# A two-layer encoder trunk on one core: three kinds of transposes issued later

## The chip, the cores and the metric

The kernel runs on one core of one Trainium2 chip. The metric is the device time of one execution in microseconds (us), from the core's first to its last work; lower is better.

## The reference

Two layers of a bidirectional encoder over 256 tokens of width 1024, all in float32. Each layer:

```
h = rms_norm(x)
c_q, c_kv, k_rope, dq, dk, dv = split(h @ w_in)
o_a = mla_attention(...)     # 8 heads: softmax of (q_nope k_nope + q_rope k_rope), times v
o_b = diff_attention(...)    # 8 heads: softmax map 1 minus lambda times softmax map 2, times v
merged = sigmoid(h @ w_gate)[a] * (o_a @ w_branch_a) + sigmoid(...)[b] * (o_b @ w_branch_b)
x = x + merged @ w_out
h = rms_norm(x)
x = x + swiglu(h)                      # layer 0: dense, 2816 wide
x = x + top-2-of-8 expert swiglu(h)    # layer 1: each expert 3584 wide
```

## The kernel before

**Weights in two parts.** Weights stream from HBM in float32, 1 MB at a time: 'pieces' (ring of 6 buffers) in attention and the dense layer, 'granules' (ring of 14) in the expert layer. Each is split on the chip into a high part (ScalarE copies it, `hi`, L1114; `high`, L1493) and a low part (VectorE subtracts, `lo`, L1603; `low`, L2201). A product is three matmuls of 128 x 512 per block of 128 rows of the contraction: high x high, low x high, high x low (`three`, L551 for pieces, L968 for granules). There are 4 high buffers for pieces and 6 for granules, and a high buffer is free again when TensorE has used it.

**Five queues written by hand.** TensorE, ScalarE, VectorE, GpSimd and the DMA queue of SyncE each have their own program, in which the instructions stand in a fixed order and wait on semaphores. TensorE's results lie in eight PSUM banks; `bank_table` gives every result, in advance, a bank and a number in that bank's order. A result may be written when the bank's earlier user has been read (`take`: wait for `free[bank]`); who reads it last drains its engine and then frees the bank (`gave`, L1101 on ScalarE, L1589 on VectorE). Transposed things use the banks trans0 and trans1 in turn, in the order of the list `turned`.

**The attention loop.** After a first part, TensorE runs steps u = 1 to 15 for 16 heads (u below 8: the first attention; from 8: the differential one). Step u: scores of head u; first half of a projection (`half(u, 0)`, 12 matmuls); transposes of head u - 1's probabilities (`turn_prob`, job W(u-1)); second half of the projection; then `weigh(u - 1)`, the product of turned probabilities and values, into bank ctx (job C). ScalarE in step u: copies or squares from the step before, one `hi`, the exponentials of head u (`exps`), the copy of the turned probabilities out of PSUM (`turned_prob(u - 1)`, L1244). VectorE: `low_oa` (L1846), the row maxima (`top`), one `lo`, the division (`weights`).

**The later heads' operands.** Queries and keys for the later heads (qn1, dq1, dk1) are projected inside this loop, scaled by VectorE into the buffer zb, and then turned by TensorE in two jobs of four 128 x 128 transposes each (a and b, through `turn_z`, which calls `turn`; the transposes are at L583). ScalarE copies both out (`turned_op`, L1204). Before, both jobs stand in one step directly behind W(u-1): qn1 in u = 2, dq1 in u = 4, dk1 in u = 8. Job b has the same bank as W(u-1).

**The expert loop.** Rows routed to an expert are gathered by a matrix G of ones and zeros, and the result is scattered by its transpose S. An expert has 7 chunks; step s: `project(0, s)` (gate, granules first_gran(s) and the next), transposes of the hidden chunk before (`turn`, L1002), `project(1, s)` (up, two granules), `down(s - 1)` (two granules). Each of the three is 24 matmuls. Step 0 has no turn and no down and uses granules 0 to 3; step 1 uses 4 to 7 for the projections and 8 and 9 for down. VectorE's order in step s is: low of the two down granules, low of the next step's first, `turned(s - 1)` (L2207, which down(s - 1) waits for), low of the second, low of the third, `hidden` (L2216), low of the fourth. Steps 0 and 1 of the first expert stand ahead of the loop. Between them TensorE computes the slot columns (L546, `first_columns`; VectorE reads them at L2161 and L2162 and drains at L2163) and turns G (`scatter_matrix`, L956), both in bank proj2; ScalarE copies S (L1483) in the same place. S is first used at the first expert's end.

Of the kernel before, what the change touches and what calls it, by code (L numbers as in the profile page):

```python
# [100 lines left out]
def bank_table():  # L101

    jobs, used = {}, {b: 0 for b in BANKS}

    def put(l, bank, *names):
        for name in names:
            jobs[l, name] = (bank, used[bank])
            used[bank] += 1

    def turns(l, which):  # L110
        put(l, "trans0", which + "0")
        put(l, "score0", which + "1")
        put(l, "trans0", which + "2")
        put(l, "score1", which + "3")

    for l in range(DEPTH):
        turns(l, "x")
        put(l, "proj0", "cq.0", "qr.0", "kn1.0")
        put(l, "proj1", "cq.1", "qr.1", "kn1.1")
        put(l, "proj2", "kv.0", "dk0.0", "qn0.0", "dv0.0")  # L120
        put(l, "ctx", "kv.1", "dk0.1", "qn0.1", "dv0.1", *(f"C{u}" for u in range(2 * HEADS)), "b0.1", "o1.0")
        put(l, "score0", "dq0.0", "v0.0", "v1.0", "kn0.0")
        put(l, "score1", "dq0.1", "v0.1", "v1.1", "kn0.1")
        for h in range(HEADS):
            put(l, f"score{h % 2}", f"S{h}")
        for d in range(HEADS):
            put(l, "score0", f"E{d}.0")
            put(l, "score1", f"E{d}.1")
        n = 2
        for name in ("qn1", "dq1", "dv1", "dk1", "g0", "g1", "g2", "g3", "a0"):  # L130
            for t in range(TT):
                put(l, f"proj{n % 3}", f"{name}.{t}")
                n += 1
        put(l, "proj2", "a1.0")
        put(l, "score0", "a1.1")
        put(l, "score1", "b0.0")
        put(l, "proj0", "b1.0")
        put(l, "proj1", "b1.1")
        put(l, "proj2", "o1.1")
        turned = ["KV", "KR", "cqa", "cqb", "dq0a", "dq0b", "dk0a", "dk0b", "qn0a", "qn0b", "qra", "qrb", "kn0a",  # L140
                  "kn0b", "kn1a", "kn1b"]
        for u in range(2 * HEADS):
            turned += [f"W{u}"] + {1: ["qn1a", "qn1b"], 3: ["dq1a", "dq1b"], 7: ["dk1a", "dk1b"]}.get(u, [])
        turned += ["ob0", "ob1", "ob2", "ob3", "m0", "m1", "m2", "m3"]
        for n, name in enumerate(turned):
            put(l, f"trans{n % 2}", name)
        put(l, "score0", "o0.0")
        put(l, "score1", "o0.1")
        turns(l, "f")
        if l % 2 == 0:  # L150
            n = 0
            for c in range(FF_CHUNKS):
                for m in "gu":
                    for t in range(TT):
                        put(l, f"proj{n % 3}", f"ff{m}{c}.{t}")
                        n += 1
                put(l, "trans0", *(f"h{c}.{j}" for j in range(2 if c < FF_CHUNKS - 1 else 1)))
            put(l, "score0", "acc0.0")
            put(l, "score1", "acc0.1")
            put(l, "trans1", "acc1.0")  # L160
            put(l, "ctx", "acc1.1")
        else:
            put(l, "trans1", "logit")
            put(l, "proj2", "rank")
    return jobs, used
# [10 lines left out]
def along(k, rnd, per_rnd, e=0, per_e=0):  # L176
    v = k
    for reg, per in ((rnd, per_rnd), (e, per_e)):
        v = v + reg * per if isinstance(reg, int) else reg * per + v
    return v  # L180
# [25 lines left out]
def bank_use(bank, k, rnd, e=0):  # L206
    per_rnd, per_e = MOE_USES[bank]
    return along(MOE_START[bank] + k, rnd, per_rnd, e, per_e)
# [5 lines left out]
def build(nc, x_rows, pos_row, pos_col, const, gains, lam_vecs, w_pre, ffn_row, w_router, w_exp, out, h_rows):  # L214
    with ExitStack() as ctx:
# [307 lines left out]
        def _(pe):  # L523
# [79 lines left out]
            def turn_z(l, z, job, blocks):  # L603
                if z == "qr":
                    pe.wait_ge(rotated_q, l + 1)
                else:
                    pe.wait_ge(scaled, nth(SCALED, l, z))
                turn(l, job, blocks_of(zbuf(l, z), blocks))
# [4 lines left out]
            def attention(l):  # L613
# [33 lines left out]
                def turn_both(name):  # L647
                    turn_z(l, name, name + "a", (0, 1))
                    turn_z(l, name, name + "b", (2, 3))
# [40 lines left out]
                def weigh(u):  # L690

                    pe.wait_ge(probT_ready, l * 2 * HEADS + u + 1)
                    o = open_(l, f"C{u}")
                    if u < HEADS:
                        pe.wait_ge(value, nth(VALUES, l, f"v{u // 4}.1"))
                        for k in range(TT):
                            m = mm(o[:, 0:T], blk(v_mla[:, k], u), probT[:, u % 2, k], k, TT)
                    else:
                        d = u - HEADS
                        pe.wait_ge(value, nth(VALUES, l, f"dv{d // 4}.1"))  # L700
                        for q in range(TT):
                            for k in range(TT):
                                m = mm(o[:, q * P:(q + 1) * P], probT[:, u % 2, k, q * P:(q + 1) * P],
                                       blk(v_diff[:, k], d), k, TT)
                    m.then_inc(full["ctx"], 1)
# [62 lines left out]
                def half(u, part):  # L768
                    name, t = beside[u - 1]
                    proj(name, part, t, rows_of.get(name, h))  # L770

                last = 2 * HEADS - 1
                for u in range(1, last + 1):
                    if u >= HEADS:
                        scores(u)
                    elif u % 2 == 0:
                        pair_scores(u)
                    if u == last:
                        pe.wait_ge(oa_ready, l * HEADS + HEADS)
                    half(u, 0)  # L780
                    turn_prob(u - 1)
                    for v, name in ((2, "qn1"), (4, "dq1"), (8, "dk1")):
                        if u == v:
                            turn_both(name)
                    half(u, 1)
                    weigh(u - 1)
                half(last + 1, 0)
                turn_prob(last)
# [163 lines left out]
            def scatter_matrix(value):  # L952

                o = take("proj2", value)
                for t in range(TT):
                    m = nc.tensor.transpose(o[:, t * P:(t + 1) * P], G[:, t], c_("ident"))  # L956
                m.then_inc(full["proj2"], 1)
# [9 lines left out]
            def experts(rnd):  # L967
# [81 lines left out]
                def first_columns():  # L1049
                    slot_columns(along(1, rnd, EXPERTS), bank_use("proj2", 0, rnd))  # L1050
# [6 lines left out]
                step(0, 0)  # L1057
                if first_round(rnd):
                    first_columns()
                scatter_matrix(bank_use("proj2", 1, rnd))  # L1060
                step(1, 0)
                with pe.Fori(0, EXPERTS - 1) as e:
                    for s in range(2, EXP_CHUNKS + 2):
                        step(s, e)
# [27 lines left out]
        def _(act):  # L1092
# [126 lines left out]
            def attention(l):  # L1219
# [116 lines left out]
                for u in range(1, 2 * HEADS):  # L1336
                    if 2 <= u < HEADS + 2:
                        high_oa(u - 2)
                    if u >= HEADS + 2:
                        ob_sums(u - 2 - HEADS)  # L1340
                    if u == 1:
                        squares(l, "qn1")
                    if u in (2, 3):
                        squares(l, "dq1", (u - 2,))
                    if u in (4, 5):
                        diff_values(1, u - 4)
                    if u in (6, 7):
                        squares(l, "dk1", (u - 6,))
                    if u >= HEADS:
                        gate_rows((u - HEADS) // TT, u % TT)  # L1350
                    hi(at + 16 + u)
                    for v, name in ((1, "qn1"), (3, "dq1"), (7, "dk1")):
                        if u == v:
                            roots_of(l, name)
                    exps(u)
                    turned_prob(u - 1)
                    if u == 2:
                        turned_op(l, "qn1", qnT, "qn", 4)
                    if u == 4:
                        turned_op(l, "dq1", dqT, "dq", 4)  # L1360
                    if u == 8:
                        turned_op(l, "dk1", dkT, "dk", 4)
                last = 2 * HEADS - 1
                ob_sums(HEADS - 2)
# [115 lines left out]
            def scatter_matrix(value):  # L1480

                o = fresh("proj2", value)
                A(S[:], o[:, 0:T], ACT.Copy).then_inc(scatter_ready, 1)  # L1483
                act.drain().then_inc(free["proj2"], 1)

            def experts(rnd):
# [56 lines left out]
                gathered(lambda bank: bank_use(bank, 0, rnd))  # L1543
                high(3, 0)
                step(0, 0)
                scatter_matrix(bank_use("proj2", 1, rnd))
                step(1, 0)
                with act.Fori(0, EXPERTS - 1) as e:
                    for s in range(2, EXP_CHUNKS + 2):
                        step(s, e)  # L1550
# [898 lines left out]
```

## Time and profile before

| | |
|---|---|
| median of 3 runs | 1805.65 us (1804.97 to 1808.34) |
| the profiled execution | 1804.76 us, span of its instructions 1802.9 us |
| matmuls (PE) | 1743.7 us busy, 97% of the span |
| weight loads (PEld, beside the matmuls) | 1433.7 us, 80% |
| VectorE (DVE) | 1416.0 us, 79% |
| ScalarE (ACT) | 1175.9 us, 65% |
| GpSimd (POOL) | 28.5 us, 2% |
| mean granted TensorE clock | 0.990 of full speed |
| read from HBM | 477 MB, 266 GB/s over the span |

A row of a timeline gives start, duration, engine, line of the kernel, operation, output and inputs with the program's names, shapes, and how many instructions are merged in it; in brackets, the engine's idle time before it and what ended that. ACTq and DVEq are the two engines' queues, here their drains. Times are counted from the first instruction.

### The profile page before, as it was taken

The page shows a single profiled execution, that of the slowest core. Times are in us where ns is not written, and L with a number is a line of the kernel's source. Part 1 is how long each engine was busy: PE and PEld are TensorE (multiplying, and loading weights), DVE is VectorE, ACT ScalarE, POOL GpSimd, SP SyncE. Part 2 cuts the span into 40 slices and gives each one's busy share as a digit, 9 for nine tenths or more (in the row PEclk, how much of TensorE's full clock was granted, in tenths as well). Part 3 has the DMA queues.
Part 4 walks back from the last instruction along what each step waited for, and adds up shares of the span by engine and source line. Part 5 has one row for each costly group of instructions (what it writes and reads, how often), then busy time and mean ns, then how long its engine had stood idle before and what let it go on. Part 6 is the DMA issues. An engine that isn't in the chain of part 4 may idle for free.

```text
span 1802.9 us, 23755 instructions
## 1 busy us (share of the span) xinstructions
PE 1743.7 (97%) x8220; PEld 1433.7 (80%) x8220; DVE 1416.0 (79%) x1423; ACT 1175.9 (65%) x1242; POOL 28.5 (2%) x27
## 2 busy tenths in 40 slices
PE   7999999999999999988999999999999999999997
PEld 6777878888887778776888888888888888888885
DVE  7776876544478668668889889898898998988984
ACT  7655665434466656646777777777777777777772
POOL 0200000000002000000000000000000000000000
PEclk9999999999999999989999999999999999999998
DMA  7433345555454324577999999999999999999980
GB/s 281 164 117 117 117 142 186 187 191 185 166 187 164 117 94 141 222 284 294 375 376 356 376 358 355 381 355 370 367 357 380 373 354 377 352 369 371 361 318 25
DMA packets 68408, 480.50 MB, mean 267 GB/s; under 512 B 7920, under 2 KB 8176, under 8 KB 11248
## 3 DMA queue, kind: packets, MB, share of 16 engines
q1 hardware_dynamic: 67328, 475.91, 71.0%
q0 software_dynamic: 1008, 3.67, 0.6%
q8 instruction: 41, 0.67, 0.1%
q14 instruction: 31, 0.25, 0.0%
HBM read 477.45 MB, written 2.10 MB: 266 GB/s over the span
## 4 chain that ended last, share of the span: by engine, by line
PE 77%; DVE 8%; issue 5%; ACT 4%; DVEq 4%; ACTq 1%; DMA 1%; SPq 0%
PE ps_proj L970 9%; PE ps_proj L974 9%; PE ps_proj L973 9%; PE ps_proj L552 7%; PE ps_proj L554 7%; PE ps_proj L555 7%; PE ps_score L970 5%; PE ps_score L974 5%; PE ps_score L973 5%; DVE w_raw_r L2201 3%; PE ps_score L546 2%; PE ps_trans L583 2%; PE ps_ctx L546 2%; PE ps_score L552 1%; PE ps_score L555 1%
## 5 line engine op out<-in xcount | busy, mean ns | idle before, releaser
L2201 DVE TENSOR_TENSOR w_raw_r<-w_raw,hi 128x2048 fp32r<-128x2048 f32 x336 | 759.3, 2290 | 95.1 <-ACT hi L1493 74.3
L1493 ACT ACTIVATE hi<-w_raw 128x2048 fp32r<-128x2048 f32 x335 | 639.6, 1919 | 183.3 <-PE ps_score L974 72.1
L970 PE MATMUL ps_proj<-hi,he_hi 128*128 128x512 f32 x896 | 355.3, 397 | 0.1
L974 PE MATMUL ps_proj<-w_raw_r,he_hi 128*128 128x512 f32 x896 | 350.1, 391 | 0.0
L973 PE MATMUL ps_proj<-hi,he_lo 128*128 128x512 f32 x896 | 349.6, 390 | 0.0
L1114 ACT ACTIVATE hi<-raw 128x2048 fp32r<-128x2048 f32 (+1 forms) x114 | 215.8, 1893 | 124.8 <-PE ps_proj L554 60.6
L1603 DVE TENSOR_TENSOR raw_r<-raw,hi 128x2048 fp32r<-128x2048 f32 (+1 forms) x114 | 257.2, 2266 | 33.3 <-ACT hi L1114 27.0
L552 PE MATMUL ps_proj<-hi,hT_hi 128*128 128x512 f32 (+2 forms) x496 | 198.2, 400 | 6.6 <-DVEq L1589 3.5
L974 PEld LDWEIGHTS ps_proj<-w_raw_r,he_hi 128*128 128x128 f32 x896 | 168.5, 188 | 36.1
L970 PEld LDWEIGHTS ps_proj<-hi,he_hi 128*128 128x128 f32 x896 | 168.7, 188 | 34.9 <-issue 1.5
L973 PEld LDWEIGHTS ps_proj<-hi,he_lo 128*128 128x128 f32 x896 | 168.8, 188 | 33.4
L555 PE MATMUL ps_proj<-raw_r,hT_hi 128*128 128x512 f32 (+2 forms) x496 | 190.2, 383 | 0.0
L554 PE MATMUL ps_proj<-hi,hT_lo 128*128 128x512 f32 (+2 forms) x496 | 189.9, 383 | 0.0
L970 PE MATMUL ps_score<-hi,hidT_hi 128*128 128x512 f32 x448 | 176.0, 393 | 1.6 <-DVE hidT_lo L2207 1.6
L974 PE MATMUL ps_score<-w_raw_r,hidT_hi 128*128 128x512 f32 x448 | 174.6, 390 | 0.0
L973 PE MATMUL ps_score<-hi,hidT_lo 128*128 128x512 f32 x448 | 174.4, 389 | 0.0
L552 PEld LDWEIGHTS ps_proj<-hi,hT_hi 128*128 128x128 f32 x496 | 94.2, 190 | 31.4 <-issue 12.9
L555 PEld LDWEIGHTS ps_proj<-raw_r,hT_hi 128*128 128x128 f32 x496 | 93.9, 189 | 18.7
L554 PEld LDWEIGHTS ps_proj<-hi,hT_lo 128*128 128x128 f32 x496 | 94.3, 190 | 15.9
L970 PEld LDWEIGHTS ps_score<-hi,hidT_hi 128*128 128x128 f32 x448 | 84.1, 188 | 19.2 <-DVE hidT_lo L2207 2.3
L974 PEld LDWEIGHTS ps_score<-w_raw_r,hidT_hi 128*128 128x128 f32 x448 | 84.1, 188 | 17.7
L973 PEld LDWEIGHTS ps_score<-hi,hidT_lo 128*128 128x128 f32 x448 | 84.2, 188 | 17.1
(347 smaller groups left out, 2000.7 us busy)
## 6 DMA issues: line engine op xcount, KB each, us to landing
w_raw<-in_w_exp SPq DMA_DIRECT2D x336, 1024.0 KB, 6.7
raw<-in_w_pre SPq DMA_DIRECT2D x110, 1024.0 KB, 4.9
raw<-in_w_pre SPq DMA_DIRECT2D x4, 640.0 KB, 6.0
x_tok<-in_x_rows SPq DMA_DIRECT2D x2, 512.0 KB, 4.9
raw<-in_w_pre SPq DMA_DIRECT2D x2, 512.0 KB, 5.9
h_rows<-htok SPq DMA_DIRECT2D x1, 1024.0 KB, 8.2
out_rows<-x_tok SPq DMA_DIRECT2D x1, 1024.0 KB, 4.1
grow<-in_ffn_row SPq DMA_DIRECT2D x1, 512.0 KB, 5.7
```

The lines of the kernel that those rows point to most:

```text
L546: m = nc.tensor.matmul(o, lhsT, rhs, start=(k == 0), stop=(k == n - 1))
L552: m = nc.tensor.matmul(o, x_h, w_h, start=first, stop=False)
L554: m2 = nc.tensor.matmul(o, x_l, w_h, start=False, stop=False)
L555: return m2, nc.tensor.matmul(o, x_h, w_l, start=False, stop=last)
L583: m = nc.tensor.transpose(o[:, b * P:(b + 1) * P], src, c_("ident"))
L970: m = nc.tensor.matmul(o, a_hi, w_h, start=first, stop=False)
L973: nc.tensor.matmul(o, a_lo, w_h, start=False, stop=False)
L974: return nc.tensor.matmul(o, a_hi, w_l, start=False, stop=last)
L1114: A(high[g % HIGH][:, 0:w], raw[g % RAW][:, 0:w], ACT.Copy).then_inc(piece_hi, 1)
L1493: A(w_hi[k % HS][:], w_raw[n], ACT.Copy).then_inc(gran_hi, 1)
L1603: V.tensor_tensor(low[g % RAW][:, 0:w], raw[g % RAW][:, 0:w], high[g % HIGH][:, 0:w].bitcast(F32), ALU.subtract).then_inc(piece_lo, 1)
L2201: V.tensor_tensor(w_low[k % WS], w_raw[k % WS], w_hi[k % HS][:].bitcast(F32), ALU.subtract)\
```

## The change

Three edits. In the attention loop, job b of a turned chunk moves from before the second half of the step's projection to behind it, for qn1, dq1 and dk1 alike. Both jobs of dk1, and their copies on ScalarE, move from u = 8 to u = 9, and their place in the banks' order with them. In the expert part, TensorE's turn of G and ScalarE's copy of S move from between steps 0 and 1 to behind step 1. No instruction is added or removed.

```diff
--- before.py
+++ after.py
@@ -140,7 +140,7 @@
         turned = ["KV", "KR", "cqa", "cqb", "dq0a", "dq0b", "dk0a", "dk0b", "qn0a", "qn0b", "qra", "qrb", "kn0a",
                   "kn0b", "kn1a", "kn1b"]
         for u in range(2 * HEADS):
-            turned += [f"W{u}"] + {1: ["qn1a", "qn1b"], 3: ["dq1a", "dq1b"], 7: ["dk1a", "dk1b"]}.get(u, [])
+            turned += [f"W{u}"] + {1: ["qn1a", "qn1b"], 3: ["dq1a", "dq1b"], 8: ["dk1a", "dk1b"]}.get(u, [])
         turned += ["ob0", "ob1", "ob2", "ob3", "m0", "m1", "m2", "m3"]
         for n, name in enumerate(turned):
             put(l, f"trans{n % 2}", name)
@@ -779,10 +779,12 @@
                         pe.wait_ge(oa_ready, l * HEADS + HEADS)
                     half(u, 0)
                     turn_prob(u - 1)
-                    for v, name in ((2, "qn1"), (4, "dq1"), (8, "dk1")):
-                        if u == v:
-                            turn_both(name)
+                    turned = {2: "qn1", 4: "dq1", 9: "dk1"}.get(u)
+                    if turned:
+                        turn_z(l, turned, turned + "a", (0, 1))
                     half(u, 1)
+                    if turned:
+                        turn_z(l, turned, turned + "b", (2, 3))
                     weigh(u - 1)
                 half(last + 1, 0)
                 turn_prob(last)
@@ -1057,8 +1059,8 @@
                 step(0, 0)
                 if first_round(rnd):
                     first_columns()
+                step(1, 0)
                 scatter_matrix(bank_use("proj2", 1, rnd))
-                step(1, 0)
                 with pe.Fori(0, EXPERTS - 1) as e:
                     for s in range(2, EXP_CHUNKS + 2):
                         step(s, e)
@@ -1358,7 +1360,7 @@
                         turned_op(l, "qn1", qnT, "qn", 4)
                     if u == 4:
                         turned_op(l, "dq1", dqT, "dq", 4)
-                    if u == 8:
+                    if u == 9:
                         turned_op(l, "dk1", dkT, "dk", 4)
                 last = 2 * HEADS - 1
                 ob_sums(HEADS - 2)
@@ -1543,8 +1545,8 @@
                 gathered(lambda bank: bank_use(bank, 0, rnd))
                 high(3, 0)
                 step(0, 0)
+                step(1, 0)
                 scatter_matrix(bank_use("proj2", 1, rnd))
-                step(1, 0)
                 with act.Fori(0, EXPERTS - 1) as e:
                     for s in range(2, EXP_CHUNKS + 2):
                         step(s, e)
```

## Rows read from the trace of the kernel before

**Rows 1.** stretches of the span: busy us of each engine (instructions), granted clock, DMA share, GB/s
```profile
84.00:90.00 6.00, 5.60 (x29) 4.76 (x30) 4.40 (x5) 2.17 (x5) 0.78 (x1) 1.00 0.54 178
...
176.00:179.80 3.80, 3.10 (x10) 2.65 (x11) 1.88 (x7) 1.89 (x4) 0.00 (x0) 0.55 0.19 78
...
900.00:1790.00 890.00, 885.58 (x4034) 728.72 (x4033) 788.37 (x506) 649.64 (x441) 5.62 (x6) 1.00 0.92 350
```

**Rows 2.** TensorE's waits: for whom, us in total, times, longest
```profile
PE ps_trans L583 <- ACTq L1101: 8.1, 6, 3.3
...
PE ps_proj L956 <- DVEq L2163: 7.3, 1, 7.3
```

**Rows 3.** timeline of TensorE, layer 0: start us, us, instruction [idle before, releaser]
```profile
84.40 0.47 PE L552 MATMUL ps_proj<-hi,hT_hi 128*128 128x512 f32 x1 [1.80 <-DVEq L1589]
```

**Rows 4.** timeline of TensorE, layer 0, u = 8 and the scores of u = 9
```profile
172.37 0.60 PE L583 MATMUL ps_trans<-cst,prob 128*128 128x128 f32 x4
...
176.70 1.09 PE L583 MATMUL ps_trans<-cst,zb 128*128 128x128 f32 x4 [3.29 <-ACTq L1101]
...
181.33 1.02 PE L546 MATMUL ps_ctx<-probT,v_mla 128*128 128x256 f32 x4
...
182.29 1.14 PE L546 MATMUL ps_score<-dkT,dqT 64*128 64x256 f32 x8
```

**Rows 5.** timeline of ScalarE and VectorE, layer 0, u = 8 and 9
```profile
175.94 0.57 ACT L1244 ACTIVATE probT<-ps_trans 128x512 f32<-128x512 f32 x1
...
182.39 0.38 ACT L1249 ACTIVATE oaT_hi<-ps_ctx 128x256 fp32r<-128x256 f32 x1 [3.88 <-PE ps_ctx L546]
...
182.88 0.42 DVE L1846 TENSOR_TENSOR oaT_lo<-ps_ctx,oaT_hi 128x256 fp32r<-128x256 f32 x1 [4.85 <-ACT oaT_hi L1249]
...
188.45 0.58 ACT L1244 ACTIVATE probT<-ps_trans 128x512 f32<-128x512 f32 x1
```

**Rows 6.** timeline of TensorE, layer 0, u = 9: W8 and weigh(8)
```profile
186.21 0.60 PE L583 MATMUL ps_trans<-cst,dprob 128*128 128x128 f32 x4
...
189.40 1.05 PE L546 MATMUL ps_ctx<-v_diff,probT 128*128 128x128 f32 x8
```

**Rows 7.** timeline of TensorE and ScalarE, layer 0, u = 2
```profile
121.74 0.60 PE L583 MATMUL ps_trans<-cst,zb 128*128 128x128 f32 x4
...
122.72 0.63 PE L583 MATMUL ps_trans<-cst,zb 128*128 128x128 f32 x4 [0.38 <-ACTq L1101]
...
123.10 0.47 PE L552 MATMUL ps_proj<-hi,hT_hi 128*128 128x512 f32 x1
...
126.99 0.38 ACT L1249 ACTIVATE oaT_hi<-ps_ctx 128x256 fp32r<-128x256 f32 x1 [2.85 <-PE ps_ctx L546]
```

**Rows 8.** timeline of TensorE, the experts' steps 0 and 1
```profile
817.70 0.50 PE L546 MATMUL ps_proj<-pair,G 128*128 128x2 f32 x4
...
825.48 0.69 PE L956 MATMUL ps_proj<-cst,G 128*128 128x128 f32 x2 [7.28 <-DVEq L2163]
...
838.44 0.39 PE L970 MATMUL ps_score<-hi,hidT_hi 128*128 128x512 f32 x1
...
843.88 0.39 PE L970 MATMUL ps_proj<-hi,he_hi 128*128 128x512 f32 x1
```

**Rows 9.** timeline of VectorE, the experts' steps 0 and 1
```profile
815.54 6.69 DVE L2201 TENSOR_TENSOR w_raw_r<-w_raw,hi 128x2048 fp32r<-128x2048 f32 x3
...
822.97 2.29 DVE L2201 TENSOR_TENSOR w_raw_r<-w_raw,hi 128x2048 fp32r<-128x2048 f32 x1
...
828.77 6.70 DVE L2201 TENSOR_TENSOR w_raw_r<-w_raw,hi 128x2048 fp32r<-128x2048 f32 x3 [3.10 <-ACT hi L1493]
...
835.39 0.68 DVE L2207 TENSOR_TENSOR hidT_lo<-ps_trans,hidT_hi 128x512 fp32r<-128x512 f32 x1
...
841.44 6.89 DVE L2201 TENSOR_TENSOR w_raw_r<-w_raw,hi 128x2048 fp32r<-128x2048 f32 x3
```

**Rows 10.** timeline of ScalarE, the experts' step 0
```profile
813.17 5.52 ACT L1493 ACTIVATE hi<-w_raw 128x2048 fp32r<-128x2048 f32 x3
```

## Prediction

> **What bounds the kernel now.** I read the page's table of engines first: matmuls cover 97% of the span, VectorE 79%, ScalarE 65%. Then a table of stretches: between 900 and 1790 us TensorE is busy 885.6 of 890 us at full granted clock, VectorE 788, while the DMA engines are busy 0.92 of the time [rows 1]. So almost every microsecond is TensorE's own work, and a change that removes no matmul can only win where TensorE stands still or runs at the lower of its two clocks (1.2 instead of 2.4 GHz). The list of TensorE's waits says where that is: six waits of the zb and probability transposes for a ScalarE drain, 8.1 us together, the longest 3.3, and one of 7.3 us of the scatter matrix for VectorE [rows 2]. The diff touches just these. In the whole trace no engine waits for DMA but the first transposes for x, so time saved early isn't lost to loading later.
>
> A wait costs more than its length if it lowers the clock. After the 3.29 us wait the granted clock is 0.55 for 3.8 us; after one of 1.80 us it stays 1.00 [rows 1, 3].
>
> **The chunk dk1, u = 8 (once in each layer; layer 0 shown, layer 1 has the same 3.29 us).** Before: W7 is turned at 172.37, dk1a 0.43 us later, then dk1b needs the bank that W7 holds. ScalarE copies W7 only after the four exponentials of step 8, at 175.94 for 0.57 us, and dk1b starts at 176.70. weigh(7) starts at 181.33 and the scores of step 9 at 182.29 [rows 4, 5].
> After, u = 8 has no dk1. A turn of W and a half projection behind it take 189.40 - 186.21 = 3.19 us at full clock [rows 6], so TensorE is at weigh(7) at 172.37 + 3.19 = 175.56. weigh(7) reads the same copy, which is there at 176.51, say 176.6 with its handover: a new wait of 1.0 us, below the 1.80 that kept the clock. Then 0.96 us of weigh (182.29 - 181.33), and the scores of step 9 start at 177.56: 4.73 us earlier. That is the 3.29, 1.4 us of slow clock (176.70 to 182.29 is 5.59 us, where 0.38 + 2.83 + 0.96 = 4.17 would do, the 0.38 from [rows 7]) and one turn, less the new 1.0.
>
> u = 9 gets both turns. Everything on ScalarE and VectorE there starts from weigh(7): ScalarE sat idle 3.88 us before its copy of C7, VectorE 4.85 us before low_oa(7), so it was free from 178.03; moved up by 4.73 us that instruction starts at 178.15, which just fits [rows 5]. W8 is turned at 181.48, dk1a follows (+0.43), then the half projection: 181.48 + 0.43 + 3.19 = 185.1, and TensorE is at dk1b. dk1b needs W8's bank: its copy at 188.45 + 0.58 becomes 184.3. So it doesn't wait, by 0.8 us. The two turns add 0.43 + 0.38 = 0.8 us. ScalarE copies dk1b by about 186.2, under weigh(8), and then would wait for weigh(8)'s output anyway. Net 4.73 - 0.8 = 3.9 us per layer, **7.8 us** for both. The heads of dk1 are read first at u = 12, three steps later. Nothing of this issues a DMA; SP's queue waits for used pieces and follows TensorE.
> Bounds: if the 1.0 us wait also cost the clock, 1.2 to 1.4 us less per layer (11.4 us as the total below); if it were nil, 1.0 more per layer.
>
> **qn1 at u = 2 and dq1 at u = 4 (four places in both layers).** Before, the first turn starts at 121.74, the second at 122.72 (after 0.38 us of wait for W1's bank), and the projection at 123.10: 1.36 us. Apart, each turn costs 0.38 us, 0.76 together, and the second finds its bank free, which it came to be at 122.7. Saved 0.6 us. The cost is that ScalarE stands in its queue for the second turn until about 125.4 and copies it until 126.1; it was idle 2.85 us before 126.99, waiting for weigh(1), which comes behind that turn and takes 0.9 us, so the copy lies under it [rows 7]. dq1 shows the same times. 4 x 0.6 = **2.4 us**; bounds 0 (the copy of 0.69 us lands on ScalarE's path each time) and 2.6.
>
> **The scatter matrix.** Before, TensorE ends step 0 with the columns product at 817.70 and waits 7.28 us, to 825.48, for the drain behind VectorE's slot_columns, which VectorE reaches only after granules 4 to 7. Then the first projection of step 1, and down(0) starts at 838.44, step 2 at 843.88 [rows 8].
> After, TensorE goes straight into step 1 at about 818.1. Its granules: VectorE makes 4, 5 and 6 in three instructions from 815.54 (done 817.8, 820.0, 822.2), and 7 from 822.97 to 825.26 [rows 9]. A projection is 24 matmuls like down(0), which takes 843.88 - 838.44 = 5.44 us. The first runs to 823.6, the turn to 823.9, the second to 829.4, none of it late. down(0) then waits for turned(0) on VectorE. That stood at 835.39 for 0.68 us, behind granules 8 to 10, which began at 828.77 after 3.10 us of idling for ScalarE's copy of granule 8. ScalarE had ended its copies 5 to 7 at 813.17 + 5.52 = 818.69 and then stood at the scatter matrix, which TensorE turns at 825.48 [rows 8 to 10]; now it goes on at once, so VectorE loses just those 3.10 us and turned(0) ends at 836.07 - 3.10 = 832.97. So **the wait isn't removed but half of it moves to down(0): 829.4 to 833.0, 3.6 us**. down(0) takes its 5.44 us, the scatter matrix 0.38.
> Without loss of clock step 2 starts at 833.0 + 5.44 + 0.38 = 838.8, 5.1 us earlier. But 3.6 us is more than the 3.29 us that cost 1.4 us in both layers, so I take that: 840.2, a gain of **3.7 us**.
> The Trainium skill (TensorE: Matmul & The Clock Gate, section on the HAM clock gate) says that the gate's observation is free-running, not aligned with the kernel; by that a wait near the edge may escape, and the sum would be 5.1. The two equal rows here don't show such an escape.
> What is late next: ScalarE's copy of S now stands behind step 1, so granule 14 waits for TensorE's scatter turn: free at 840.6, copies 14 to 16 until 846.4. VectorE then makes 14, 15, 16 by 849.3 and turned(1) by 850.0. TensorE wants it at 840.2 + 5.46 + 0.44 + 5.46 = 851.5: 1.5 us to spare, where before it was over 3 (four granules from 841.44 and turned(1), about 851.7, against 843.88 + 11.3 = 855.2). VectorE has 788 of 890 us to do in the loop [rows 1], so it gains some 1.5 us per step and the margin grows. SP's refills wait for gran_done, so they too come earlier; they run at 350 GB/s with no consumer waiting. GpSimd's first gather needs the second index, far later.
>
> **Sum.** 7.8 + 2.4 + 3.7 = 13.9 us. The profiled execution took 1804.76 us (span 1802.9): 1790.9. It lies 0.9 us under the median of the runs, 1805.65, so I forecast **1791.7**, 0.8% faster. No change can be told within 0.2%, or 3.6 us.
>
> **The rivals.**
> 1. *No clock is lost at down(0)*, the wait of 3.6 us escaping: 5.1 for 3.7, 1790.3. For it: nothing between 1.8 and 3.29 us was seen. Against: 3.29 did cost, twice.
> 2. *The new wait at weigh(7) is longer or lowers the clock*: 2.5 to 2.9 us less, and with the copies of qn1 and dq1 on ScalarE's path up to 2.4 less, 1794 to 1797. For it: low_oa(7) fits by only 0.1 us, dk1b by 0.8. Against: the 1.80 us wait at full clock.
> 3. *The gain is spent again in the expert loop*: granule 14 is late, VectorE's margin of 1.5 us is gone and TensorE waits at down(1), down(2) until VectorE has caught up. If copies or handovers are 2 us later than I have it, some 1 to 3 us come back: 1793 to 1795.
> 4. *Slower*: the expert loop settles in a worse order, in which TensorE waits for turned() in each step because ScalarE waits for TensorE. Over the 55 steps left it takes 0.25 us per step to eat 13.9 us; 0.4 us per step would give 1814. For it: each of the three engines waits for the next one. Against: VectorE's 100 us of spare time in the loop [rows 1], which is more than 1.5 us a step.
> 5. *Nothing*: the waits are only moved to the next dependency in all places, as happens to half of the scatter wait: 1803 to 1806. Against: weigh(7) depends on one copy whose time is on the trace.
>
> **How the numbers follow.** Forecast with rival 1, which differ by 1.4 us: 0.68. Rival 2: 0.12; rival 3: 0.11; rival 5: 0.04; rival 4: 0.03; something else, either side, 0.02. Both signs don't share the chance, so one range: downward no new wait at weigh(7) and no lost clock (2.0 + 1.4 us, and 0.9 us for the runs), 1787.5; upward rivals 2 and 3, 1797.5. Faster by over 0.2%: 0.93; within: 0.04; slower: 0.03.
>
> **What will show it.** Right: no wait of a zb transpose for a ScalarE drain; TensorE idle about 1.0 us before ps_ctx of weigh(7) in both layers, clock kept; scores of step 9 near 176.4 (177.56 less 1.2 us of the earlier turns); no wait of 7 us at the scatter matrix, but one of 3.6 us of ps_score (down) for hidT_lo with a clock of about 0.5 behind it; the expert loop as long as before. Wrong: a wait at dk1b in u = 9, ScalarE late at oaT_hi, hidT_lo waits in steps 2 to 4, or a loop that is longer from step to step.

## The result

The changed kernel takes 1791.88 us (median of 4 runs, 1789.35 to 1794.02) against 1805.31 us (4 runs, 1803.53 to 1808.34): ratio 0.992, 95% interval 0.9908 to 0.9932. That is 13.4 us faster. The forecast was 1791.7 us. The profiled execution has a span of 1787.5 us, 15.4 less than the one before. It is the fastest of the four.

TensorE's waits after, of the whole span. The two groups of [rows 2] are gone, and two others are new or longer:

```profile
PE ps_score L972 <- DVE hidT_lo L2209: 5.3, 3, 3.7
...
PE ps_ctx L546 <- ACT probT L1246: 1.7, 2, 0.9
```

The copy of the turned probabilities is waited for once in each layer, 0.85 us, and hidT_lo at down(0) for 3.66 us (its other two waits, 1.6 us together, are the ones of the kernel before).

TensorE in layer 0, u = 8 and 9, its transposes, scores and weigh (these answer to [rows 4, 6]):

```profile
171.27 0.60 PE L583 MATMUL ps_trans<-cst,prob 128*128 128x128 f32 x4
...
175.48 1.13 PE L546 MATMUL ps_ctx<-probT,v_mla 128*128 128x256 f32 x4 [0.85 <-ACT probT L1246]
...
176.54 1.14 PE L546 MATMUL ps_score<-dkT,dqT 64*128 64x256 f32 x8
...
180.47 0.60 PE L583 MATMUL ps_trans<-cst,dprob 128*128 128x128 f32 x4
...
180.90 0.60 PE L583 MATMUL ps_trans<-cst,zb 128*128 128x128 f32 x4
...
184.11 0.60 PE L583 MATMUL ps_trans<-cst,zb 128*128 128x128 f32 x4
...
184.54 1.06 PE L546 MATMUL ps_ctx<-v_diff,probT 128*128 128x128 f32 x8
```

W7 is turned at 171.27 and nothing stands between it and the half projection. weigh(7) waits 0.85 us, the scores of u = 9 start at 176.54. W8 is turned at 180.47, dk1a at 180.90, dk1b at 184.11 without a wait.

ScalarE and VectorE there, against [rows 5]:

```profile
174.85 0.57 ACT L1246 ACTIVATE probT<-ps_trans 128x512 f32<-128x512 f32 x1
...
176.64 0.38 ACT L1251 ACTIVATE oaT_hi<-ps_ctx 128x256 fp32r<-128x256 f32 x1 [1.22 <-PE ps_ctx L546]
...
177.13 0.42 DVE L1848 TENSOR_TENSOR oaT_lo<-ps_ctx,oaT_hi 128x256 fp32r<-128x256 f32 x1 [0.20 <-ACT oaT_hi L1251]
...
182.69 0.57 ACT L1246 ACTIVATE probT<-ps_trans 128x512 f32<-128x512 f32 x1
...
184.75 0.69 ACT L1206 ACTIVATE dkT<-ps_trans,gn 128x512 f32<-128x512 f32 x1 [0.68 <-PE ps_trans L583]
```

ScalarE's copies of W7 and W8 end at 175.42 and 183.26, VectorE reaches low_oa(7) with 0.20 us to spare instead of 4.85, and ScalarE copies dk1b under weigh(8).

u = 2 in layer 0, TensorE and then ScalarE, against [rows 7]:

```profile
125.08 0.60 PE L583 MATMUL ps_trans<-cst,zb 128*128 128x128 f32 x4
...
125.52 1.03 PE L546 MATMUL ps_ctx<-probT,v_mla 128*128 128x256 f32 x4
...
125.72 0.69 ACT L1206 ACTIVATE qnT<-ps_trans,gn 128x512 f32<-128x512 f32 x1 [2.23 <-PE ps_trans L583]
...
126.58 0.39 ACT L1251 ACTIVATE oaT_hi<-ps_ctx 128x256 fp32r<-128x256 f32 x1 [0.18 <-PE ps_ctx L546]
```

The second job stands alone at 125.08, weigh(1) follows 0.44 us later, and ScalarE, busy with the copy until 126.4, is still 0.18 us early for the output of weigh(1). That margin was 2.85.

TensorE at the experts' steps 0 and 1, against [rows 8]: the columns product, down(0) and the start of step 2.

```profile
807.64 0.50 PE L546 MATMUL ps_proj<-pair,G 128*128 128x2 f32 x4
...
823.33 0.47 PE L972 MATMUL ps_score<-hi,hidT_hi 128*128 128x512 f32 x1 [3.66 <-DVE hidT_lo L2209]
...
829.03 0.48 PE L972 MATMUL ps_proj<-hi,he_hi 128*128 128x512 f32 x1
```

VectorE and ScalarE there, against [rows 9, 10]:

```profile
815.78 6.69 DVE L2203 TENSOR_TENSOR w_raw_r<-w_raw,hi 128x2048 fp32r<-128x2048 f32 x3
...
822.39 0.68 DVE L2209 TENSOR_TENSOR hidT_lo<-ps_trans,hidT_hi 128x512 fp32r<-128x512 f32 x1
...
832.00 6.70 DVE L2203 TENSOR_TENSOR w_raw_r<-w_raw,hi 128x2048 fp32r<-128x2048 f32 x3 [1.26 <-ACT hi L1495]
...
838.61 0.68 DVE L2209 TENSOR_TENSOR hidT_lo<-ps_trans,hidT_hi 128x512 fp32r<-128x512 f32 x1
...
803.11 10.93 ACT L1495 ACTIVATE hi<-w_raw 128x2048 fp32r<-128x2048 f32 x6
...
829.31 0.39 ACT L1485 ACTIVATE S<-ps_proj 128x256 fp32r<-128x256 f32 x1 [3.50 <-PE ps_proj L958]
```

ScalarE makes its six high copies without a stop, VectorE goes from granule 7 to granules 8 to 10 with no idle time, and turned(0) ends at 823.07. From the columns product to step 2 it takes 21.39 us instead of 26.18. VectorE waits 1.26 us for granule 14, whose copy stands behind that of S, and turned(1) still ends at 839.3, before TensorE's down(1), which starts at 840.5.

Two stretches after; the columns are those of [rows 1]. The first holds the wait at down(0), and the clock stays 1.00. The second is the expert loop, TensorE busy 880.6 of 885 us: nothing is given back there.

```profile
806.00:831.00 25.00, 21.34 (x99) 17.34 (x99) 24.06 (x16) 16.11 (x12) 0.00 (x0) 1.00 0.82 311
...
890.00:1775.00 885.00, 880.59 (x4010) 724.65 (x4009) 784.61 (x504) 645.41 (x438) 5.64 (x6) 1.00 0.92 350
```

### The profile page after: what moved, and what is told of

Same layout as the page of the kernel before. It is cut to its first block, busy times and chain, and to the rows that moved or that the text cites. A ratio compares the mean times of both kernels' runs of the same rounds, so it can differ in the third digit from the quotient of the medians.

```text
span 1787.5 us, 23755 instructions
## 1 busy us (share of the span) xinstructions
PE 1738.2 (97%) x8220; PEld 1429.4 (80%) x8220; DVE 1415.6 (79%) x1423; ACT 1175.3 (66%) x1242; POOL 28.5 (2%) x27
## 4 chain that ended last, share of the span: by engine, by line
PE 77%; DVE 8%; issue 5%; ACT 4%; DVEq 4%; ACTq 1%; DMA 1%; SPq 0%
PE ps_proj L972 9%; PE ps_proj L976 9%; PE ps_proj L975 9%; PE ps_proj L552 7%; PE ps_proj L555 7%; PE ps_proj L554 7%; PE ps_score L972 5%; PE ps_score L976 5%; PE ps_score L975 5%; DVE w_raw_r L2203 3%; PE ps_score L546 2%; PE ps_trans L583 2%; PE ps_ctx L546 2%; PE ps_score L552 1%; PE ps_score L555 1%
```

## The experiments

Every experiment was timed beside the kernel before, 4 to 8 times, and profiled once. In the tables 'to step 2' is the time from the columns product to the start of step 2, and 'down(0)' from its first matmul to step 2. Where the scatter matrix is turned behind step 1, that is down(0), 5.44 us in the trace before, and its two transposes.

### Each part alone

The attention edits alone: in the changed kernel the scatter matrix goes back between steps 0 and 1, in both TensorE's and ScalarE's program.

```diff
-                step(1, 0)
                 scatter_matrix(bank_use("proj2", 1, rnd))
+                step(1, 0)
```

> The changed kernel with the scatter matrix back between steps 0 and 1, so only the attention edits are made. By my sum these are worth 10.0 us (the two traces show 5.0 and 5.1 us per layer), so about 10 us faster than the kernel before, with the 7.3 us wait at the scatter matrix and its slow clock back. Rival (the time is given back in the expert part): under 7 us.

The scatter matrix alone: the kernel before with this edit, in both programs.

```diff
-                scatter_matrix(bank_use("proj2", 1, rnd))
                 step(1, 0)
+                scatter_matrix(bank_use("proj2", 1, rnd))
```

> The kernel before with only the scatter matrix moved behind step 1. If the wait of 3.6 us at down(0) costs the clock, 3.7 us faster than before; if it does not, 4.8 to 5.1 us. Rival (the parts are not independent, the expert part gains only because it starts in another phase): the two parts alone do not add up to the whole, 13.4 us, within 2 us.

| kernel | median us | ratio to before (95%) |
|---|---|---|
| before, same chip | 1805.71 | |
| attention edits alone | 1795.9 | 0.9941 (0.9928 to 0.9953) |
| scatter matrix alone | 1802.31 | 0.9977 (0.9966 to 0.9987) |

By the medians 9.8 and 3.4 us, together 13.2, against 13.4 for the whole. The intervals leave 8.5 to 13.0 and 2.3 to 6.1 us, so within the noise the parts add up, and no loss of the attention part in the expert part shows. In the trace of the scatter matrix alone down(0) starts like this:

```profile
833.67 0.77 PE L970 MATMUL ps_score<-hi,hidT_hi 128*128 128x512 f32 x1 [3.65 <-DVE hidT_lo L2207]
...
834.23 0.63 PE L973 MATMUL ps_score<-hi,hidT_lo 128*128 128x512 f32 x1
...
841.78 0.48 PE L970 MATMUL ps_proj<-hi,he_hi 128*128 128x512 f32 x1
```

The wait is the same as in the changed kernel, 3.65 us. But here the matmuls behind it are 0.43 us apart instead of 0.23, the lower clock, and down(0) to step 2 takes 8.11 us instead of 5.70.

### The clock at down(0)

The changed kernel was run unaltered two more times.

> The changed kernel again, unaltered, for a second profile and more times. Forecast by my sum: the wait at down(0) of 3.6 us lowers the clock in some executions, then down(0) to step 2 takes about 7.2 us instead of the 5.7 us of the first profile. Rival: a wait of that length never costs the clock, and it takes 5.7 us again.

> The changed kernel once more, for a direct comparison and a third profile of down(0): with its clock kept, 21.4 us from the columns product to step 2; lost, 23.8 us. Three of five profiles with a wait of 3.6 us have lost it wholly or in part, so 1791 to 1792 us as the median either way.

Median 1791.35 us (ratio 0.9917, 0.9905 to 0.993) and 1791.64 us (0.9912, 0.9896 to 0.9927). down(0) and step 2 in the first of them:

```profile
825.06 0.47 PE L972 MATMUL ps_score<-hi,hidT_hi 128*128 128x512 f32 x1 [3.65 <-DVE hidT_lo L2209]
...
830.76 0.48 PE L972 MATMUL ps_proj<-hi,he_hi 128*128 128x512 f32 x1
```

and in the second, with one row inside:

```profile
825.25 0.47 PE L972 MATMUL ps_score<-hi,hidT_hi 128*128 128x512 f32 x1 [3.63 <-DVE hidT_lo L2209]
...
826.25 0.39 PE L975 MATMUL ps_score<-hi,hidT_lo 128*128 128x512 f32 x1
...
826.47 0.58 PE L976 MATMUL ps_score<-w_raw_r,hidT_hi 128*128 128x512 f32 x1
...
832.58 0.48 PE L972 MATMUL ps_proj<-hi,he_hi 128*128 128x512 f32 x1
```

In the first the clock is kept, 5.70 us. In the second the first five matmuls run at full clock, the sixth and those behind it at half: 7.33 us, and 22.99 us to step 2. Over all six profiles with this wait:

| profile | wait us | down(0) us | to step 2 us |
|---|---|---|---|
| changed kernel | 3.66 | 5.70 | 21.39 |
| again | 3.65 | 5.70 | 21.37 |
| third time | 3.63 | 7.33 | 22.99 |
| scatter matrix alone | 3.65 | 8.11 | 23.78 |
| dk1 in u = 8 (below) | 3.65 | 8.13 | 23.80 |
| dk1's jobs together (below) | 3.62 | 7.12 | 22.76 |

The same wait costs nothing, 1.4 to 1.6 us, or 2.4 us. Between 3.62 and 3.66 us the length doesn't decide.

The same chance stands in a shorter wait, near the start of layer 0, in all kernels here: that of [rows 3]. In the first profile of the changed kernel, and then in the second:

```profile
84.54 0.47 PE L552 MATMUL ps_proj<-hi,hT_hi 128*128 128x512 f32 x1 [1.80 <-DVEq L1591]
```

```profile
84.55 0.47 PE L552 MATMUL ps_proj<-hi,hT_hi 128*128 128x512 f32 x1 [1.85 <-DVEq L1591]
...
86.42 0.63 PE L554 MATMUL ps_proj<-hi,hT_lo 128*128 128x512 f32 x1
```

with, in the second, this stretch (columns of [rows 1], granted clock 0.50):

```profile
86.00:88.00 2.00, 2.00 (x6) 1.61 (x5) 2.00 (x2) 0.00 (x0) 0.00 (x0) 0.50 1.00 295
```

In the first the clock stays at 1.00, and from this matmul to the next scores (at 99.48) it takes 14.94 us; in the second it falls after five matmuls and takes 16.53, in the third 16.63. Over the 13 profiles of this document the wait measures 1.78 to 1.86 us; it left the clock in five (the kernel before is one) and lowered it in eight. This accounts, to some 0.3 us, for how the three profiles of the unaltered kernel differ: the span is 1787.5 us with no loss at either wait, 1789.4 with a loss here alone, and 1791.1 with a loss here and at down(0).

To see what a longer wait at down(0) does, VectorE got extra work ahead of granule 8, additions into a buffer whose content is overwritten later:

```diff
+                    if s == 1:
+                        for _ in range(2):
+                            V.tensor_tensor(y_lo[:], x_tok[:, 0], x_tok[:, 1], ALU.add)
+                            dve.drain()
                     if s:
                         low(down0, e)
```

> The changed kernel with two additions of 128 x 1024 (and a drain each, about 2.4 us together) on VectorE before granule 8, with a result nobody reads. The wait at down(0) grows to about 6 us. If the clock is lost there by chance at 3.65 us (kept in two profiles, lost in two), at 6 us it should always be lost: 2.4 us more plus 2.4 us of slow clock, so 3 to 5 us slower than the changed kernel. If the length does not matter: 2.4 us slower, and the clock sometimes kept. If VectorE's work there is hidden after all: no change.

Median 1795.61 us (0.9941, 0.9927 to 0.9954), about 4 us above the changed kernel's 1791.35 to 1791.88. The wait grew to 6.18 us and the slow clock is there from the first matmul:

```profile
828.26 0.76 PE L972 MATMUL ps_score<-hi,hidT_hi 128*128 128x512 f32 x1 [6.18 <-DVE hidT_lo L2209]
...
836.58 0.47 PE L972 MATMUL ps_proj<-hi,he_hi 128*128 128x512 f32 x1
```

8.32 us from down(0) to step 2. The two additions take 2.5 us and the wait is 2.5 us longer, so VectorE's work ahead of turned(0) sets this wait microsecond by microsecond. One profile can't show that the clock is always lost at 6 us. Of the 4 us, 2.5 are the work; that the other 1.5 are a clock lost more often or for longer is an estimate from the difference.

### Which of the two attention edits brings the gain

dk1 back in u = 8, its second job still behind the half projection:

```diff
-        ... 8: ["dk1a", "dk1b"]
+        ... 7: ["dk1a", "dk1b"]
-                    turned = {2: "qn1", 4: "dq1", 9: "dk1"}.get(u)
+                    turned = {2: "qn1", 4: "dq1", 8: "dk1"}.get(u)
-                    if u == 9:
+                    if u == 8:
                         turned_op(l, "dk1", dkT, "dk", 4)
```

> The changed kernel with dk1 back in u = 8, but its second job still behind the half projection. Theory A (the delay of dk1 by a step is what brings the gain): the second job waits for W7's bank again and most of 3.3 us per layer returns, some 6 us slower than the changed kernel. Theory B (the gain comes from the half projection now standing between the jobs; weigh(7) waits for the same copy anyway): the second job waits 0.6 us, weigh(7) no more, and the time is that of the changed kernel, 0.3 us per layer less at best.

Median 1791.37 us (0.991, 0.9897 to 0.9924): the changed kernel's time, though this profile lost the clock at down(0). TensorE at u = 8: dk1a, dk1b, weigh(7), scores of u = 9.

```profile
173.63 0.60 PE L583 MATMUL ps_trans<-cst,zb 128*128 128x128 f32 x4
...
177.53 0.63 PE L583 MATMUL ps_trans<-cst,zb 128*128 128x128 f32 x4 [0.54 <-ACTq L1103]
...
177.99 1.03 PE L546 MATMUL ps_ctx<-probT,v_mla 128*128 128x256 f32 x4
...
178.95 1.14 PE L546 MATMUL ps_score<-dkT,dqT 64*128 64x256 f32 x8
```

dk1b waits 0.54 us for the bank, and weigh(7) then doesn't wait at all, because the copy that frees the bank is the copy that weigh(7) reads. Theory A has fallen: once the jobs stand apart, the step's delay brings nothing.

Both jobs of dk1 in u = 9, together before the half projection:

```diff
                         turn_z(l, turned, turned + "a", (0, 1))
+                    if u == 9:
+                        turn_z(l, turned, turned + "b", (2, 3))
                     half(u, 1)
-                    if turned:
+                    if turned and u != 9:
                         turn_z(l, turned, turned + "b", (2, 3))
```

> The changed kernel with both dk1 jobs before the second half of the projection in u = 9. If it is the half projection between the jobs that hides W8's copy, the second job waits about 2.5 us for the ScalarE drain (copy of W8 done at 183.3 on the changed kernel's trace, TensorE there at 181.3, less what the clock does), 2 to 3.5 us slower per layer, 4 to 7 us in all. If moving dk1 by a step is enough by itself, no wait and the changed kernel's time.

Median 1795.75 us (0.9947, 0.9933 to 0.9961), 4 us slower than the changed kernel. The second job waits again:

```profile
181.07 0.60 PE L583 MATMUL ps_trans<-cst,zb 128*128 128x128 f32 x4
...
183.61 0.63 PE L583 MATMUL ps_trans<-cst,zb 128*128 128x128 f32 x4 [1.94 <-ACTq L1105]
```

From the scores of u = 8 to those of u = 10 in layer 0:

| kernel | us |
|---|---|
| before | 21.94 |
| dk1's jobs together in u = 9 | 20.29 |
| changed | 18.18 |
| second job behind the half, dk1 in u = 8 | 17.82 |

With the jobs together, the delay by a step gives 1.65 us: the wait is 1.94 instead of 3.29 us and the clock is kept. With the half projection between the jobs the whole gain is there in either step.

### A better kernel: turned(0) first

In step 1 ahead of the loop VectorE makes turned(0) before the second down granule, where it stood behind two more:

```diff
                     if s:
                         low(down0, e)
...
+                    early = s == 1
+                    if early:
+                        turned(s - 1, e)
                     if s:
                         low(down0 + 1, e)
...
                     low(next0, e)
-                    if s:
+                    if s and not early:
                         turned(s - 1, e)
```

> The changed kernel with VectorE making turned(0) before granule 9 instead of behind granule 10, in step 1 ahead of the loop only. If the wait of 3.65 us at down(0) is VectorE's order, it goes (turned(0) ready at 818.9, TensorE there at 819.3), the clock stays, and some 1.3 us come back at down(1), where VectorE then is short: 2 to 2.5 us faster than a run of the changed kernel that kept its clock, 4 to 5 us faster than one that lost it. Rival (granules 9 to 11 are then too late, all of it comes back): the changed kernel's time.

Median 1788.51 us (0.9904, 0.9888 to 0.9919). The wait at down(0) is gone, 17.44 us to step 2, and down(1) waits 0.89 us. With dk1 in u = 8 besides:

> Turned(0) first, as in the run before, and dk1 in u = 8 with the half projection between its jobs, which gave the changed kernel's time. A candidate for a better kernel: about 1788 to 1789 us, and by the traces 0.5 us less than with dk1 in u = 9.

> The kernel of turned(0) first and dk1 in u = 8, unaltered, on the chip of its neighbours: 1787 us again, 3 to 5 us under the changed kernel. Rival (its lead was chance of the clock): within 1.5 us of the changed kernel.

1787.26 us (0.9896, 0.9881 to 0.9912), and once more 1787.03 us (0.9887, 0.9871 to 0.9902), beside the changed kernel's 1791.64 on the same chip: 4.6 us less. It beats both kernels. VectorE in the last profile, granule 8, turned(0) and granules 9 to 12:

```profile
815.04 2.29 DVE L2203 TENSOR_TENSOR w_raw_r<-w_raw,hi 128x2048 fp32r<-128x2048 f32 x1
...
817.25 0.68 DVE L2209 TENSOR_TENSOR hidT_lo<-ps_trans,hidT_hi 128x512 fp32r<-128x512 f32 x1
...
818.08 8.90 DVE L2203 TENSOR_TENSOR w_raw_r<-w_raw,hi 128x2048 fp32r<-128x2048 f32 x4
```

turned(0) ends at 817.93, 11.03 us behind the start of the columns product; in the first profile of the changed kernel it is 15.43. down(1) then waits 1.37 us for turned(1):

```profile
837.35 0.49 PE L972 MATMUL ps_score<-hi,hidT_hi 128*128 128x512 f32 x1 [1.37 <-DVE hidT_lo L2209]
```

VectorE works there without a gap (granules 9 to 12 and 13 to 16 are each back to back), so this is its work, not ScalarE's copy of S. Against the changed kernel with its clock kept this gives 21.39 - 17.44 = 4.0 us at step 2 and takes 1.4 back. That is 2.6 of the 4.6 us. dk1 in u = 8 gives 0.35 us a layer in the traces, 0.7; the last 1.3 are by elimination the clock that the changed kernel often loses at down(0), where this kernel has no wait.

If the earlier place is good once, is it in every step?

```diff
-                    early = s == 1
+                    early = s >= 1
```

> The best kernel so far with turned(s - 1) ahead of the second down granule in every step of the expert loop, not in step 1 alone. If the wait at down(1) (1.36 us in the last profile) is the order alone, it goes and the time is 1 to 1.5 us lower. Rival: in the loop VectorE runs ahead of TensorE, and an earlier turned() makes it wait for ScalarE's copy of a product that TensorE has not made yet; its lead is lost in each of 56 steps and it becomes slower, by 0.1 us a step some 6 us.

Median 1845.73 us (1.0207, 1.0193 to 1.0221): 2% slower than the kernel before, 58.7 us slower than with the order changed in one step. Both branches of the expectation missed: the rival had the direction and the reason, but put it at some 6 us, at 0.1 us a step. TensorE's waits, whole span:

```profile
PE ps_proj L972 <- DVE he_lo L2187: 20.2, 7, 2.9
...
PE ps_ctx L546 <- DVEq L2197: 13.5, 8, 1.9
...
PE ps_ctx L546 <- DVE y_lo L2176: 9.5, 8, 1.8
```

and VectorE's, between 860 and 1800 us:

```profile
DVE hidT_lo L2209 <- ACT hidT_hi L1507: 115.3, 44, 6.8
```

VectorE stands at turned() 44 times, 115 us in all, for ScalarE's copy of a hidden chunk that TensorE has yet to turn. Its lead is then missing where an expert ends and the next begins: there TensorE waits for he_lo, for y_lo and for the banks of the output, 43.2 us together. Of that 41.1 us lie in the loop. Behind nine of these waits the granted clock fell as well. An estimate of what this costs is, for each stretch of 5 us between 860 and 1830 us, 5 us times the missing share of the clock: 17 us in all, and 0 in the kernel without this edit. With 1.6 us at the 1.80 us wait near the start, which lowered the clock here and not in the last profile of the best kernel, that is 59.7 of the 60.0 us between the two spans.

## Why the prediction was right

**The second jobs of qn1 and dq1.** Forecast 0.6 us each. From the scores of u = 2 to those of u = 8 it took 51.05 us before and 49.82 after, in both layers: 0.62 each. ScalarE's copy did hide under weigh, with 0.18 us left.

**dk1.** Forecast 3.9 us per layer with a new wait of 1.0 us at weigh(7) and the clock kept. Measured 21.94 - 18.18 = 3.76 and in layer 1 3.85, the wait 0.85, the clock kept. The step was right in its parts and in the fear that it fits closely: low_oa(7) by 0.20 us. The sentence that takes the 4.73 us apart doesn't add up: 3.29 + 1.4 + 0.4 - 1.0 is 4.1, because two turns leave u = 8 and not one. The 4.73 itself is a difference of two times and came out as 4.66 (13.85 us between the scores of u = 8 and u = 9 before, 9.19 after), and the two turns cost u = 9 0.90 us where 0.8 was forecast. What the prediction didn't see is that the move to u = 9 isn't needed. The two dependencies of u = 8 end in one copy, so a turn put into that wait is nearly free, while in u = 9 it costs its full 0.43 us. The premise for a kept clock was also too strong: the prediction took 1.80 us as a length that keeps the clock, and the same wait lowered it in eight of 13 profiles. That the wait at weigh(7) did no harm rests on its being shorter: at 0.85 to 0.86 us the clock stayed in both layers of all seven profiles that have it.

**The scatter matrix.** That half of the wait moves to down(0) was right to 0.1 us (3.6 forecast, 3.66 found), and its mechanism was shown by lengthening the wait and by taking it away. Without a loss of clock the sum said 5.1 us and the first profile has 26.18 - 21.39 = 4.8: down(0) starts 0.26 us behind the end of turned(0), a handover that the sum left out. The mis-sized term is the clock's loss: put at 1.4 us after the rows at 3.29 us, it is 0, 1.4 to 1.6, or 2.4 us. The gain was therefore 4.8 us in the first profile, which is rival 1, and 2.4 to 3.4 us in those that lost the clock, where 3.7 was forecast. The medians of the changed kernel, 1791.35 to 1791.88, fit a mixture of executions that lose the clock at down(0), at the 1.8 us wait, at both or at neither. So the forecast is within 0.2 us of the measured time partly by luck: the attention parts were right to 0.2 us (7.8 and 2.4 forecast, 7.6 and 2.5 in the traces), but the scatter part is 2.4 to 4.8 where 3.7 was forecast, and the chance of the clock alone moves an execution by up to 3.6 us, the difference of the profiled spans. The Trainium skill (TensorE: Matmul & The Clock Gate, section on the HAM clock gate) says that the gate's observation isn't aligned with the kernel. The table of six profiles agrees, with 5.70 to 8.13 us behind waits that differ by 0.04 us, but no run moves the wait alone, so that this is the reason isn't shown.

**The rivals.** The new wait at weigh(7) lowering the clock (2) and the gain spent in the loop (3) didn't occur: the loop from step 2 on is as long as before, 948.4 us from there to the start of TensorE's last matmul against 948.7. The slower rival (4) was no feature of this change, and no run shows it as written. The kernel with turned() early in every step does settle in a worse order, 58.7 us slower, but there TensorE waits where an expert ends and not for turned() in each step. The rival that all waits only move (5) holds for the 0.85 and the 3.66 us. One reading was wrong without consequence: the prediction says that only TensorE's first transposes wait for a DMA, but in the trace before ScalarE also waits twice for its first pieces, 2.8 us in all, before 18 us.

**The span.** The first profiles differ by 15.4 us: 10.05 at the router, 14.85 at step 2, 15.4 at the end, the last half microsecond because the final products ran at a higher clock after than before: behind a wait of 1.76 us and one of 0.34 the kernel before lost it, and the changed kernel didn't.

```profile
1789.61 0.50 PE L546 MATMUL ps_ctx<-y_hi,S 128*128 128x512 f32 x1 [1.76 <-DVE y_lo L2174]
...
1791.15 0.80 PE L546 MATMUL ps_ctx<-y_hi,S 128*128 128x512 f32 x1 [0.34 <-DVEq L2195]
```

The medians differ by 13.4. The profiled execution is the fastest of its four and lost the clock at neither wait; the other three weren't profiled, but the two later profiles of the same kernel show such losses at 1.85, 1.81 and 3.63 us.

## What to carry to other kernels

When two waits stand one behind the other, find what each ends on: if it is the same instruction, put independent work between them, and moving one to another step adds nothing. Before moving a waiting instruction, list in order what the slower engine still has to do for the next consumer; here that gave the new wait to 0.1 us, and pointed to the one instruction to pull forward. Before explaining a difference of one or two microseconds between two single profiles, compare the granted clock behind each wait of both: a kernel run again unaltered differed by 3.6 us in this way. An order that is right in a start-up step, where VectorE is behind, is wrong in the steady loop, where it is ahead.

## What the runs showed of the hardware

A wait of 3.62 to 3.66 us of TensorE left the clock at 2.4 GHz in two executions and lowered it to 1.2 GHz in four; in one of these only after five matmuls at full clock had run. The costs were 0, 1.4 to 1.6, and 2.4 us.

Shorter waits can lower it too. In the 13 profiles:

| wait us | where | clock fell |
|---|---|---|
| 3.29 to 3.30 | dk1b, kernel before and scatter matrix alone | 4 of 4 |
| 2.88 to 2.90 | expert ends, turned() early in every step | 6 of 7 |
| 1.92 to 1.94 | dk1's jobs together | 0 of 2 |
| 1.86 to 1.90 | expert ends, turned() early in every step | 3 of 7 |
| 1.78 to 1.86 | near the start of layer 0 | 8 of 13 |
| 1.75 to 1.76, then 0.3 | the last products | 3 of 13 |
| 1.69 to 1.71 | near the start of layer 1 | 0 of 13 |
| 1.41 | last down() | 0 of 13 |

Near the start of layer 0 the fall came after TensorE had resumed and cost 1.6 to 1.7 us. So in these kernels neither the wait of 1.8 us nor that of 3.65 us tells by its length whether the clock falls, and what decides in one execution isn't shown.
